# Block transposes and gathers in the first self-attention, and weight rounding placed ahead of some ScalarE work

## The reference, cut to what matters

```python
s = jnp.einsum('bqhd,bqkhd->bhqk', qb, k_sel).astype(jnp.float32) * (HEAD_DIM ** -0.5)
s = jnp.where(valid[:, None], s, -jnp.inf)
p = jax.nn.softmax(s, axis=-1).astype(v.dtype)
return jnp.einsum('bhqk,bqkhd->bqhd', p, v_sel)
```

## Time and profile before

| | us |
|---|---|
| median of 3 runs | 3256.46 |
| the three runs | 3250.9, 3256.46, 3260.51 |
| the profiled execution | 3252.9 |
| its span, first to last instruction | 3250.9 |
| TensorE matmul busy | 3223.4 |
| VectorE busy | 1613.1 |
| ScalarE busy | 1292.0 |
| GpSimd busy | 1570.8 |

### The profile page before, as it was taken

One profiled execution on the slowest core, in us unless ns is written; L12 is line 12 of the kernel. 1 busy time (PEld: TensorE's weight loads), 2 busy tenths in 40 slices (PEclk: granted clock), 3 DMA queues, 4 the chain that ended last, 5 costly groups with the idle time before them and its releaser, 6 DMA issues.

```text
span 3250.9 us, 40100 instructions
## 1 busy us (share of the span) xinstructions
PE 3223.4 (99%) x15156; PEld 2547.6 (78%) x15156; DVE 1613.1 (50%) x2736; ACT 1292.0 (40%) x1984; POOL 1570.8 (48%) x1224
## 2 busy tenths in 40 slices
PE   9999999999999999999999999999999999999999
PEld 7788778787877767767788888887676788888887
DVE  4566433546543678864555321227887455442020
ACT  4343643334464322454446322232235544642231
POOL 4554334545434563334463565646333446446473
PEclk9999999999999999999999999999999999999999
DMA  4323224323223523452353433334236235334332
GB/s 158 98 84 97 75 88 147 120 94 92 81 84 91 184 98 101 142 145 81 112 182 98 130 118 97 102 122 139 91 119 166 77 112 187 118 117 123 97 91 97
DMA packets 145976, 370.16 MB, mean 114 GB/s; under 512 B 18670, under 2 KB 35630, under 8 KB 145784
## 3 DMA queue, kind: packets, MB, share of 16 engines
q1 hardware_dynamic: 145784, 367.60, 37.0%
HBM read 316.02 MB, written 25.30 MB: 105 GB/s over the span
## 4 chain that ended last, share of the span: by engine, by line
PE 93%; DVE 4%; ACT 2%; issue 1%; POOL 1%; DMA 0%; SPq 0%; DVEq 0%; ACTq 0%
PE B L942 27%; PE B L944 27%; PE B L943 27%; PE B L1007 1%; PE B L1111 1%; PE B L1134 1%; PE B L1167 1%; PE B L1209 1%; PE B L1217 1%; PE B L1198 1%; POOL WSP L1732 1%; PE B L1082 1%; PE B L1073 1%; PE B L1148 1%; PE B L1203 0%
## 5 line engine op out<-in xcount | busy, mean ns | idle before, releaser
L1732 POOL TENSOR_TENSOR WSP<-WRAW,WSP 128x512 fp32r<-128x512 f32 x1036 | 1359.0, 1333 | 1469.9 <-ACT WSP L1350 1469.4
L942 PE MATMUL B<-H,WSP 128*128 128x512 f32 x2496 | 993.0, 398 | 7.7 <-POOL WSP L1732 7.7
L944 PE MATMUL B<-H,WSP 128*128 128x512 f32 x2496 | 972.6, 390 | 0.0
L943 PE MATMUL B<-H,WSP 128*128 128x512 f32 x2496 | 971.9, 389 | 0.0
L1350 ACT ACTIVATE WSP<-WRAW 128x1024 fp32r<-128x1024 f32 (+1 forms) x567 | 555.8, 984 | 669.3 <-PE B L944 528.7
L942 PEld LDWEIGHTS B<-H,WSP 128*128 128x128 f32 x2496 | 468.8, 188 | 127.6 <-issue 25.3
L943 PEld LDWEIGHTS B<-H,WSP 128*128 128x128 f32 x2496 | 469.0, 188 | 100.9 <-issue 6.9
L944 PEld LDWEIGHTS B<-H,WSP 128*128 128x128 f32 x2496 | 468.5, 188 | 99.0
L1815 DVE TENSOR_TENSOR B<-B,RN 128x512 f32<-128x512 f32 x194 | 134.8, 697 | 392.1 <-PE B L944 375.8
L942 PE MATMUL B<-YM,WSP 128*128 128x512 f32 x512 | 199.5, 390 | 0.0
L944 PE MATMUL B<-YM,WSP 128*128 128x512 f32 x512 | 199.2, 389 | 0.0
(11 more groups left out here) (451 smaller groups left out, 4806.8 us busy)
## 6 DMA issues: line engine op xcount, KB each, us to landing
WRAW<-in_wb SPq DMA_DIRECT2D x318, 512.0 KB, 3.7
WRAW<-in_wa SPq DMA_DIRECT2D x153, 512.0 KB, 3.7
PTB<-BLK SPq DMA_DIRECT2D x128, 128.0 KB, 2.7
WRAW<-in_wa SPq DMA_DIRECT2D x50, 256.0 KB, 2.6
WRAW<-in_wb SPq DMA_DIRECT2D x48, 256.0 KB, 2.6
parked<-HYT SPq DMA_DIRECT2D x24, 256.0 KB, 2.1
QA<-RXA SPq DMA_DIRECT2D x64, 64.0 KB, 2.0
xs<-PA SPq DMA_DIRECT2D x16, 256.0 KB, 4.4
```

Source lines behind the costliest of these rows:

```text
L942: e.matmul(o, L[0], R[0], start=first, stop=False)
L943: e.matmul(o, L[0], R[1], start=False, stop=False)
L944: return e.matmul(o, L[1], R[0], start=False, stop=last)
L1732: x = e.tensor_tensor(WSP[:, i % NSP, 1, c:c + CUT], WRAW[:, i % NRAW, c:c + CUT], WSP[:, i % NSP, 0, c:c + CUT].bitcast(fp32), ALU.subtract)
```

## The change

It has two parts. (1) In the first self-attention the weights of the softmax stay in a new arrangement. VectorE adds the bias in the score bank itself; ScalarE's exponential reads the bank and writes every 32nd key of a query into PA so that 32 x 32 blocks lie together; after the multiplication by the inverted sum VectorE transposes the blocks in place (unit "ablocks"), and SyncE gathers them into PTA with eight DMAs for each half of the queries (unit "agather"). The unit "tr" is gone with its transposes and copies. The score banks are four in place of two. The value product has twelve matmuls in place of eight, over the same columns. The order of the units around it is written anew, in main and in PICKS. (2) ScalarE, when it comes to a unit "sc", "qss", "gout" or "gfront" and has rounded only what was due so far, rounds the next weight before its own work of that unit.

The diff, cut (the strings of digits are left out; the order that they give is told below it):

```diff
             Unit("kbc", "a", l, c, pj=True), Unit("krope", "a", l, c)]
 
-main += qk(0)
+def sc(c, i):
+    return Unit("sc", "a", l, c, i, s=True)
+
+def nrm(c, i):
+    return Unit("nrm", "a", l, c, i)
+
+def turned(c, i):
+    return Unit("ablocks", l, c, i)
+
+nxt = qk(1)
+main += qk(0) + [sc(0, 0), *nxt[:2], nrm(0, 0), sc(0, 1), *nxt[2:4], turned(0, 0), nrm(0, 1), sc(0, 2), *nxt[4:], turned(0, 1),
+                 Unit("agather", l, 0, 0), nrm(0, 2), sc(0, 3), turned(0, 2), nrm(0, 3), turned(0, 3), Unit("agather", l, 0, 1)]
 for c in range(4):
-    nxt = qk(c + 1) if c < 3 else []
-    for i in range(4):
-        main.append(Unit("sc", "a", l, c, i, s=True))
-        main += nxt[:2]
-        nxt = nxt[2:]
-        if i:
-            main.append(Unit("tr", "a", l, c, i - 1, t=True))
-        main.append(Unit("nrm", "a", l, c, i))
-    main += nxt
-    main.append(proj("agate", l, c, src=H, w=[(*A, "agate", c)]))
-    main.append(Unit("tr", "a", l, c, 3, t=True))
-    main.append(Unit("pv", "a", l, c, o=True))
-    main += [Unit("atty", l, c), Unit("split", "YB", A, c)]
+    nxt = qk(c + 2) if c < 2 else []
+    if c:
+        main += [Unit("agather", l, c, 0), sc(c, 2), sc(c, 3), nrm(c, 2), turned(c, 2), nrm(c, 3), turned(c, 3),
+                 Unit("agather", l, c, 1)]
+    main += nxt[:2] + [proj("agate", l, c, src=H, w=[(*A, "agate", c)])]
+    if c < 3:
+        main += [sc(c + 1, 0), sc(c + 1, 1), nrm(c + 1, 0), nrm(c + 1, 1), *nxt[2:], turned(c + 1, 0), turned(c + 1, 1)]
+    main += [Unit("pv", "a", l, c, o=True), Unit("atty", l, c), Unit("split", "YB", A, c)]
 if n:
 ...
 MS, COSA, SINA = at(24, "MS", 8), at(32, "COSA", 1), at(33, "SINA", 1)
 BIAS, VA4, QA, KA = at(34, "BIAS", 3), at(37, "VA4", 4), at(41, "QA", 2), at(43, "KA", 2)
-PA, PTA, RXA, GA = at(45, "PA", 4), at(49, "PTA", 8), at(57, "RXA", 4), at(62, "GA", 3)
+PA, PTA, RXA, GA = at(45, "PA", 6), at(51, "PTA", 6), at(57, "RXA", 4), at(62, "GA", 3)
 
 ...
 def score_bank(ab, i, hh):
 
-    return (S0, S1)[hh] if ab == "a" else (S0, S1, T0, T1)[(2 * i + hh) % 4]
+    return (S0, S1, T0, T1)[(2 * i + hh) % 4]
+
+def query_half(t, h, hh):
+
+    return t[:, 2 + 2 * hh:4 + 2 * hh, :].rearrange("p s x -> p (s x)") if h else t[:, hh, :]
+
+def weights_tile(i, hh):
+
+    t = query_half(PA, i // 2, hh).rearrange("p (b j i k) -> p i b j k", b=4, i=2, k=32)
+    return t[:, i % 2, :, 0:i + 1, :]
 
 ...
         half = slice(64 * hh, 64 * hh + 64)
         if ab == "a":
-            b = take((S0, S1)[hh], dve_done, ("smax", ab, l, c, i, hh))
+            b = take(score_bank(ab, i, hh), act_done, ("exp", ab, l, c, i, hh))
             q, kk = QA[half, c % 2, 128 * i:128 * i + 128], KA[half, c % 2, 0:n]
         else:
             b = take(score_bank(ab, i, hh), act_done, ("exp", ab, l, c, i, hh))
             q, kk = QB[half, c % 2, 128 * i:128 * i + 128], KB[half, (c // 2 + hh) % 2, :]
         e.matmul(b[:, 0:n], q, kk, start=True, stop=True).then_inc(*mm_done.up(("sc", ab, l, c, i, hh)))
-elif k == "tr":
-    ab, l, c, i = a
-    nk = i + 1
-    for hh in range(2):
-        b = take((T0, T1)[hh], (dve_done, act_done)[hh], ("pt", ab, l, c, i, hh))
-        w.wait_ge(act_done, ("nrm", ab, l, c, i, hh))
-        p = PA[:, 2 * (i % 2) + hh, :]
-        turn(b, [p[:, 128 * j:128 * j + 128] for j in range(nk)], nk, ("tr", ab, l, c, i, hh))
 elif k == "pbc":
 ...
 ab, l, c = a
 b = take(O, dve_done, ("lo", "YB", ("a", l), c))
-w.wait_ge(dve_done, ("pt", ab, l, c, 3, 0))
-w.wait_ge(act_done, ("pt", ab, l, c, 3, 1))
+for h in range(2):
+    w.wait_ge(gathered[h], ("agather", l, c, h))
 w.wait_ge(act_done, ("tok", "vtok", l, 3))
-for j in range(4):
-    q0 = 128 * j
-    for hh in range(2):
-        v = VA4[:, j, 128 * c + 64 * hh:128 * c + 64 * hh + 64]
-        x = e.matmul(b[64 * hh:64 * hh + 64, q0:512], v, PTA[:, 4 * hh + j, q0:512], start=j == 0, stop=j == 3)
+for h in range(2):
+    for j in range(2 * h + 2):
+        i0 = max(2 * h, j)
+        for hh in range(2):
+            v = VA4[:, j, 128 * c + 64 * hh:128 * c + 64 * hh + 64]
+            p = query_half(PTA, h, hh).rearrange("p (r j q) -> p j r q", r=4, j=2 * h + 2)[:, j, :, 32 * (i0 - 2 * h):64]
+            o = b[64 * hh:64 * hh + 64, :].rearrange("p (i r q) -> p r i q", i=4, r=4)[:, :, i0:2 * h + 2, :]
+            x = e.matmul(o, v, p, start=j == 0, stop=j == 2 * h + 1)
 x.then_inc(*mm_done.up(("pv", *a)))
 ...
 w.wait_ge(landed, "par")
 own = [0]
+begun, done = None, 0
 for u in plan:
     k, a = u.kind, u.a
     if own[-1] != act_done.n:
         w.value(act_done.sem, own[-1])
         own.append(act_done.n)
+    if k in ("sc", "qss", "gout", "gfront") and begun.kind != "woa" and done == begun.w0 + len(begun.w) - 1:
+        done += 1
+        next_halves(done + NSP - 1)
     for g in range(len(u.w)):
-        if u.w0 + g:
-            next_halves(u.w0 + g + NSP - 1)
+        if u.w0 + g > done:
+            done += 1
+            next_halves(done + NSP - 1)
+    begun = u if u.w else begun
     if k == "nadd":
 ...
 elif k == "sc":
     ab, l, c, i = a
-    n = 128 * (i + 1) if ab == "a" else 512
     m = SM[:, 6 + i, :]
     load_table(ACT.Exp)
     w.wait_ge(dve_done, ("neg", ab, l, c, i))
+    if ab == "a" and c:
+        w.wait_ge(gathered[i // 2], ("agather", l, c - 1, i // 2))
     if ab == "b" and (c or i > 1):
         back = (c, i - 2) if i > 1 else (c - 1, i + 2)
         w.wait_ge(dve_done, ("blocks", l, *back, 1))
     for hh in range(2):
-        p = (PA if ab == "a" else PB)[:, 2 * (i % 2) + hh, 0:n]
-        s = p if ab == "a" else banks[score_bank(ab, i, hh)][:, :]
+        p = weights_tile(i, hh) if ab == "a" else PB[:, 2 * (i % 2) + hh, :]
+        s = banks[score_bank(ab, i, hh)][:, :]
+        if ab == "a":
+            s = s[:, 0:128 * (i + 1)].rearrange("p (j k b) -> p b j k", k=32, b=4)
         e.activation(p, s, ACT.Exp, bias=m[:, 2 + hh:3 + hh], scale=SM[:, 4 + c % 2, 2 * i + hh:2 * i + hh + 1],
 ...
 elif k == "nrm":
     ab, l, c, i = a
-    n = 128 * (i + 1)
     w.wait_ge(dve_done, ("rsum", ab, l, c, i))
     for hh in range(2):
-        p = PA[:, 2 * (i % 2) + hh, 0:n]
+        p = weights_tile(i, hh)
         e.activation(p, p, ACT.Copy, scale=SM[:, 6 + i, 6 + hh:7 + hh]).then_inc(
             *act_done.up(("nrm", ab, l, c, i, hh)))
-elif k == "tr":
-    ab, l, c, i = a
-    nk = i + 1
-    if i == 0 and c:
-        w.wait_ge(mm_done, ("pv", ab, l, c - 1))
-    w.wait_ge(mm_done, ("tr", ab, l, c, i, 1))
-    e.activation(PTA[:, 4:4 + nk, 128 * i:128 * i + 128],
-                 banks[T1][:, 0:128 * nk].rearrange("p (k q) -> p k q", q=128), ACT.Copy).then_inc(
-        *act_done.up(("pt", ab, l, c, i, 1)))
 elif k in ("fm1", "fm2"):
 ...
 n = 128 * (i + 1) if ab == "a" else 512
 m, q2 = SM[:, 6 + i, :], SM[:, 4 + c % 2, 2 * i:2 * i + 2]
+if (ab, c, i) == ("a", 0, 0):
+    for x in range(8 if l else 0):
+        w.wait_ge(landed, ("xs", 1, x))
+    for h, t in enumerate((PA[:, 0:2, :], PA[:, 2:6, :])):
+        ahead = t.rearrange("p s x -> p (s x)").rearrange("p (n j x) -> p j n x", n=8, j=2 + 2 * h)
+        e.memset(ahead[:, 1 + 2 * h, :, 0:32], 0.0).then_inc(*dve_done.up(("ahead", l, h)))
 if ab == "a":
     bias = BIAS[:, i - 1, 0:n] if i else causal
     if i:
         w.wait_ge(dve_done, ("bias", l, i))
-    if c or i > 1:
-        back = (c, i - 2) if i > 1 else (c - 1, i + 2)
-        w.wait_ge(mm_done, ("tr", ab, l, *back, 1))
 if c and ab == "a":
     w.wait_ge(act_done, ("nrm", ab, l, c - 1, i, 1))
 ...
     w.wait_ge(mm_done, ("sc", ab, l, c, i, hh))
     if ab == "a":
-        x = e.tensor_tensor_reduce(out=PA[:, 2 * (i % 2) + hh, 0:n], in0=b[:, 0:n], in1=bias, scale=1.0, scalar=NEG,
+        x = e.tensor_tensor_reduce(out=b[:, 0:n], in0=b[:, 0:n], in1=bias, scale=1.0, scalar=NEG,
                                    op0=ALU.add, op1=ALU.max, accum_out=m[:, hh:hh + 1])
 ...
     wide = spread_tile(c)[:, 128 * i:128 * i + 128].rearrange("p (n f) -> p n f", f=64)
     e.tensor_copy(wide, m[:, 6:8].unsqueeze(2).to_broadcast([128, 2, 64])).then_inc(*dve_done.up(("share", l, c, i)))
-elif k == "tr":
-    ab, l, c, i = a
-    nk = i + 1
-    if i == 0 and c:
-        w.wait_ge(mm_done, ("pv", ab, l, c - 1))
-    w.wait_ge(mm_done, ("tr", ab, l, c, i, 0))
-    e.tensor_copy(PTA[:, 0:nk, 128 * i:128 * i + 128],
-                  banks[T0][:, 0:128 * nk].rearrange("p (k q) -> p k q", q=128)).then_inc(
-        *dve_done.up(("pt", ab, l, c, i, 0)))
+elif k == "ablocks":
+    l, c, i = a
+    for hh in range(2):
+        p = weights_tile(i, hh)
+        w.wait_ge(act_done, ("nrm", "a", l, c, i, hh))
+        e.transpose(p, p).then_inc(*dve_done.up(("ablocks", l, c, i, hh)))
 elif k == "atty":
 ...
         w.wait_ge(landed, ("parked", l, 8 + c))
         load(G1[:, c, :], parked[l, 12 + c], ("gld", l, 1, c))
+elif k == "agather":
+    l, c, half = a
+    next_raw(coming[n_unit] + NRAW + half)
+    if half == 0 and c:
+        w.wait_ge(mm_done, ("pv", "a", l, c - 1))
```

(14 more changed lines are left out.)

## The result

| | median us | lowest to highest, runs | ratio to before, 95% interval |
|---|---|---|---|
| before | 3255.15 | 3250.9 to 3260.51, 14 | |
| changed | 3265.82 | 3262.8 to 3268.28, 14 | 1.0031 [1.0023, 1.0038] |

What follows compares the result with a forecast made beforehand. TensorE, busy 3223.4 of 3250.9 us, was taken as the bound. Terms -17.6 - 3.5 + 1.0 - 9.9 + 19.6 gave -10.4 us, from a median of 3256.46 to 3246 us; range 3224 to 3263.

Steps and rivals of the forecast that it cites:

- step 6: At kbc, TensorE waits for k factors held behind a late weight load: 19.6 us given back over two layers.
- Step 5: Rounding weights ahead on ScalarE removes four TensorE stalls: 9.9 us saved, bounds 3 to 12.
- Step 4: Extra work on VectorE and the other engines is hidden by the projections between units: put at nothing.
- Step 1: 160 attention transposes leave TensorE at 0.11 us each: 17.6 us saved, bounds 16 to 19.
- Step 2: TensorE's waits of the attention transposes go: 3.5 us saved, bounds 0 to 4.
- Step 3: Value product with twelve matmuls for eight and a strided operand: 1 us added, at most 7.
- Rival B: The DMA queue bounds: late gather blocks delay weight loads, making it slower, 3262 to 3278 us; chance 0.13.

Runs made afterwards that it cites:

- e7: The changed kernel, rounding ahead in the first self-attention only at sc (c, 2) and sc (c, 3), one more weight asked for in both halves' gathers: 3251.81 us.
- e8: As e7, but without the rounding ahead in "gout": 3252.88 us.
- e3: The kernel before with rounding ahead in all four kinds of unit, part 2 of the change alone: 3253.96 us.
- e4: The changed kernel, with SyncE asking for one more weight in the middle of the second half's gather, ahead of the exchanges: 3239.07 us.
- e9: The changed kernel without rounding ahead in the units between agate* and kbc of the first two pairs: 3243.47 us.
- e1: The changed kernel without rounding ahead in units "sc" and "qss" of the first self-attention: 3252.01 us.
- e11: The changed kernel, with one more weight asked for in the middle of the gather of both halves: 3240.69 us.
- e5: The changed kernel, rounding ahead in the first self-attention only at sc (c, 2) and sc (c, 3): 3251.35 us.

## Why the prediction was wrong, point by point

Three terms of the sum failed. The price of the waits in step 6 was their length alone, and 9.7 us of slow clock came on top, which no step has. Step 5 was to take 9.9 us of stalls away and took 5.3. Step 4 put at nothing what became 6.2 us of waits for weights.

- **Step 1** held. The rest column falls from 3221.5 to 3203.6 (the mean of the twelve without transposes), 18 us for 17.6 forecast.
- **Step 2** held: no wait of transposes for PA or its maximum is left in the changed kernel. (The "about 27 us" of waits ahead of step 1 are the span less the busy time; the waits that the view lists sum to 24.)
- **Step 3** was 1.0 us; it is nothing. From the start of the value product to the next matmul's are 416.57 - 414.26 = 2.31 us before and 2.31 us after:

```profile
414.26 2.37 PE L1148 MATMUL B<-PTA,VA 128*64 128x512 f32 x16
416.57 0.49 PE L1111 MATMUL B<-KA,QA 64*128 64x128 f32 x4
```
```profile
402.53 2.38 PE L1158 MATMUL B<-PTA,VA 128*64 128x256 f32 x24
404.84 1.34 PE L1126 MATMUL B<-KA,QA 64*128 64x384 f32 x6
```

- **Step 4** failed in one place. The new block transposes stand in VectorE's list behind top-k steps in the first pair of the first layer, so SyncE's gather starts only at 273.98 and the load behind it at 279.20; TensorE waits 3.53 us at 284.60. With the waits of 1.31 us for a weight at the end of each first attention (449.38 and 1002.85) this is 6.2 us that had been put at nothing. At 449.38 it waits for the low half of a weight that ScalarE rounded only at 445.59, behind the exponentials and multiplications of the last pair's late scores and a gate.
- **Step 5** had -9.9 us. The two stalls in the second attention and the one behind "gfront" went as said (each stretch is 2 and 1.2 us shorter). The one of 5.46 us did not go but broke up: the waits of the changed kernel at the same place are

```profile
1613.95 0.66 PE L1022 MATMUL B<-CST,GS 128*128 128x128 f32 x4 [2.23 <-ACT GS L1374]
1615.54 0.70 PE L1300 MATMUL B<-MACC,CST 128*128 128x256 f32 x2 [0.93 <-ACT KM L1384]
...
1634.97 0.47 PE L957 MATMUL B<-YBC,WSP 128*128 128x512 f32 x1 [1.76 <-POOL WSP L1741]
```

With one more of 0.47 us they are 5.4 us together, where before there were 5.46 and 0.88. From the same matmul ahead to the same one behind (1593.37 to 1622.66 before, 1608.33 to 1635.75 changed) the stretch is 1.9 us shorter, about what the slow clock behind the old stall had cost (0.54 over 4 us, 1.8 us). The lower bound of the step had named the chain that turns up again. e7 against e8 points the same way (1.1 us of median, within the intervals of both). In the first attention the step looked at no cost outside kbc; e3, which has part 2 alone, gains 5.6 us behind the first block and loses 6.8 in it, in good part because a rounding placed ahead waits for its load.
- **Step 6** was right in its mechanism and nearly in size: 23.75 for 19.6 us. For c = 1 (two layers) it forecast 6.4 and found 5.4 and 6.6. For c = 0 it forecast 3.4 and found 7.2 and 4.5: the gather started 9.3 us after the scores (forecast 7.5) in the first layer, and the k exchange took 3.5 us of the queue, not 2.4. e4 and e9 show the two halves of the cause separately: ask earlier, or don't put the rounding ahead there, and each wait is 1.6 us or less.
- **The term that was missing** is the clock. 14.9 - 5.2 = 9.7 us more are lost at 1.2 GHz; the 5 us behind each of the four stalls at kbc hold 9.2 of the 14.9. The sum priced each wait at its length. The kernel before had a row to price it from: the matmuls behind its 5.46 us stall are 0.64 us apart for each group of three instead of 0.36, 1.8 us over 4 us. With 1.8 us for each of the four waits, and as much given back at the old stall, the sum would have been -4.8; with the 9.2 us measured, -3.0. So the clock alone doesn't turn the sign.

Between the two profiled executions the forecast is -10.4 and the result +13.5, 23.9 us apart (21.1 by the medians; the profiled execution of before lies 2.3 us below its median). Clock 9.7, the weights of step 4 6.2, kbc 4.2 and step 5 4.6 (the four stretches that hold its stalls are 7.1 us shorter together, of which 1.8 are clock and already counted) make 24.7; step 3 gives 1.0 back. Rival B had the sign but not the mechanism: it needed block transposes some microseconds later than 11.3 us after the scores, and for c = 1 they were there at 11.0.

Open: why the clock sometimes falls with no wait ahead of it. In the changed kernel it is 0.58 over 384 to 388 us, and 0.71 over 348 to 352 us in the kernel before, both behind scores and sums of squares of 2 columns; other executions show it at other pairs. The other way round, the waits of 2.23 and 0.93 us behind "gout" are followed by 0.50 over 1604 to 1612 us in e3 and by 1.00 over 1613.95 to 1618.95 us in the changed kernel. This moves the clock column by some microseconds from profile to profile, and I didn't try to separate it.

## What to carry to other kernels

When an engine's list is reordered so that a prefetch step comes first, ask when that prefetch's own input is requested and by which queue: moving one load ahead of twelve other DMAs (four of the gather, eight of the exchanges) was worth 27 us here, while each half of the change alone was worth nothing that could be told. e3 shows that four exchange DMAs ahead of the load are enough to turn the prefetch into a wait. Price a stall of a busy TensorE of some 4 us and more at its length and some 2 us of slow clock (1.8 to 2.5 here), and look for such a stretch in the profile of before. Two changes that interact are to be tried as a table of both, with and without: e1 to e3 showed that the new order needs the rounding ahead at one place and is hurt by it at another.

## What the runs showed of the hardware

Waits of 4.5 us and more were followed by 1.2 GHz (a granted clock of 0.50 to 0.63 over the next 5 us in eight cases of two kernels). Below that the length of the wait alone does not tell. Behind 3.4 to 3.6 us the clock was 0.50 to 0.70 over 5 us in the six cases looked at (four in e1, one each in the changed kernel and e11); behind 3.15 us at 284.44 it stayed at 1.00 in e4, and behind 3.17 us at the same matmul of e5 it was 0.66. Behind waits of 0.2 to 1.6 us it stayed at 2.4 GHz in e4, but it was 0.66 behind 2.17 us in e3 (909.42), and in e5 0.50 over 948 to 952 us, behind a wait of 1.66 us at 944.40. Twelve matmuls with a strided operand in place of eight over the same columns took the same 2.31 us. A 128 x 512 exponential that reads a bank with a stride and writes blocks took 0.78 us, as the unstrided one did.
